# Ends of stages in an encoder layer: x copied first in the first scan step, no state in the last, feed-forward sums behind the first unit, bias rows by one product and a DMA

## What is computed

```
xn = rms_norm(x);  q, k, v, gu, gv, z, xbc, dt, gates = split(xn @ w_in)
y_a = window_attention(q, k, v, ..., rel_bias)      # bias = rel_bias[t5_bucket(key - query)], |key - query| <= 128
y_b = spatial_gating(gu, gv, ...)
y_c = ssd_branch(z, xbc, dt, ...)                   # chunked scan, forward and backward:
    # y_diag = (C B^T * decay) (x dt);  y_off = C state exp(acum);  state = state * decay + B^T (x dt decay_to_end)
h = x + (g_a * y_a @ w_up_attn + g_b * y_b @ w_up_gmlp + g_c * y_c @ w_up_ssd) @ w_out
out = h + square(relu(rms_norm(h) @ w_ff1)) @ w_ff2
```

## Time and profile before

| | us |
|---|---|
| median of 3 runs | 2508.46 |
| lowest, highest | 2508.34, 2509.58 |
| profiled execution, its time | 2509.14 |
| profiled execution, its span | 2507.3 |
| mean granted clock of PE | 0.977 of full speed |

### The profile page before, as it was taken

One profiled execution on the slowest core, in us unless ns is written; L12 is line 12 of the kernel. 1 busy time (PEld: TensorE's weight loads), 2 busy tenths in 40 slices (PEclk: granted clock), 3 DMA queues, 4 the chain that ended last, 5 costly groups with the idle time before them and its releaser, 6 DMA issues. The chain is left out here.

```text
span 2507.3 us, 33471 instructions
## 1 busy us (share of the span) xinstructions
PE 2380.2 (95%) x13080; PEld 1978.2 (79%) x13080; DVE 1109.7 (44%) x1591; ACT 857.2 (34%) x1543; POOL 155.5 (6%) x72
## 2 busy tenths in 40 slices
PE   3999999699998899999879999999999999999999
PEld 1777888576676788888768888788888888888887
DVE  4311164345654566677655543433333333333333
ACT  4431223236655444566543332421121202121120
POOL 3332343100000000000000000000000000000000
PEclk8998999899999999999989999999999999999999
DMA  3121323323223666788574341011111111111112
GB/s 120 38 84 57 123 75 125 98 86 121 92 92 101 192 198 198 217 244 243 177 254 161 91 149 48 29 42 34 42 34 42 33 42 35 40 35 40 38 38 92
DMA packets 170921, 251.04 MB, mean 100 GB/s; under 512 B 10811, under 2 KB 125755, under 8 KB 168156
## 3 DMA queue, kind: packets, MB, share of 16 engines
q1 hardware_dynamic: 170844, 249.99, 31.4%
HBM read 187.47 MB, written 62.49 MB: 100 GB/s over the span
## 5 line engine op out<-in xcount | busy, mean ns | idle before, releaser
L155 PE MATMUL acc<-r_hi,w_hi 128*128 128x512 f32 (+1 forms) x1344 | 478.4, 356 | 21.5 <-DVE r_lo L1652 16.2
L156 PE MATMUL acc<-r_hi,w_lo 128*128 128x512 f32 (+1 forms) x1344 | 477.9, 356 | 0.0
L157 PE MATMUL acc<-r_lo,w_hi 128*128 128x512 f32 (+1 forms) x1344 | 477.2, 355 | 0.0
L155 PEld LDWEIGHTS acc<-r_hi,w_hi 128*128 128x128 f32 x1344 | 255.4, 190 | 59.4 <-issue 22.1
L156 PEld LDWEIGHTS acc<-r_hi,w_lo 128*128 128x128 f32 x1344 | 255.5, 190 | 35.5
L157 PEld LDWEIGHTS acc<-r_lo,w_hi 128*128 128x128 f32 x1344 | 255.1, 190 | 35.8
L156 PE MATMUL acc<-u_hi,w_lo 128*128 128x512 f32 (+1 forms) x768 | 273.7, 356 | 0.0
L155 PE MATMUL acc<-u_hi,w_hi 128*128 128x512 f32 (+1 forms) x768 | 273.6, 356 | 0.0
L157 PE MATMUL acc<-u_lo,w_hi 128*128 128x512 f32 (+1 forms) x768 | 273.6, 356 | 0.0
L195 ACT ACTIVATE w_hi<-w_raw 128x1024 fp32r<-128x1024 f32 x119 | 124.9, 1049 | 386.2 <-PE acc L157 380.1
L155 PE MATMUL acc<-xn_hi,w_hi 128*128 128x512 f32 (+1 forms) x624 | 226.5, 363 | 13.5 <-DVE xn_lo L317 8.8
(11 more groups left out here) (204 smaller groups left out, 3481.3 us busy)
## 6 DMA issues: line engine op xcount, KB each, us to landing
w_raw<-in_w_tiles SPq DMA_DIRECT2D x146, 512.0 KB, 3.7
c_w<-s_ac SPq DMA_DIRECT2D x20, 1024.0 KB, 4.6
c_xbc<-s_xbc_T SPq DMA_DIRECT2D x20, 768.0 KB, 4.8
s_late_T<-s_l_result SPq DMA_DIRECT2D x20, 640.0 KB, 6.8
c_grown<-s_grown SPq DMA_DIRECT2D x40, 256.0 KB, 6.0
gates<-s_late_T SPq DMA_DIRECT2D x16, 512.0 KB, 3.7
s_xbc_T<-x_T_sb SPq DMA_DIRECT2D x12, 640.0 KB, 3.2
s_late_T<-la_result SPq DMA_DIRECT2D x12, 640.0 KB, 3.6
```

Source lines behind the costliest of these rows:

```text
L155: pe.matmul(out, w_hi, x_hi, start=first, stop=False)
L156: pe.matmul(out, w_lo, x_hi, start=False, stop=False)
L157: return pe.matmul(out, w_hi, x_lo, start=False, stop=last)
```

## The change

- Bias rows. The table keeps one column per head, so one product gives the rows of all heads on 8 partitions; DVE copies them once, SP stores them as `bias_row` (8x512, 16 KB) and, after the loop of six xBC tiles, has one DMA from DRAM to DRAM repeat that into `bias_rows` (`spread`). The shifted load moves from there behind the loop of four and behind `store_rows(0)`.
- First scan step. ACT copies x of step 0 before it makes the decays of step 0.
- Last scan step. x_end, kept, the state products and the state sum of step 19 are left out, y's products don't wait for the state, and group 2 of the late tile goes behind them. The last two steps leave PE's loop for that.
- Merge. The first group of `merged` is loaded by eight DMAs, each of one feature block.
- Feed-forward. `sums_of_squares` stands behind the first unit of the first tile, not behind its third.

```diff
@@ project, SP
                 for at, (lo, hi) in enumerate(zip(XBC_CUTS, XBC_CUTS[1:])):
                     kind(F_XBC + 2 * lo, 2 * (hi - lo), xbc_T[2 * lo:2 * hi], ready, 5 + 2 * lo, 1)
                     if at == 0:
-                        rb.shift(sp)
+                        rb.spread(sp)
                         store_scan()
                     else:
                         store_rows(at - 1)
+                    if at == 1:
+                        rb.shift(sp)
@@ RelativeBias
-        self.table = sb("bias_table", [NBUCKET + 1, HEADS, P])
+        self.table = sb("bias_table", [NBUCKET + 1, HEADS])
+        self.row = sb("bias_row", [HEADS, 512])
     def products(self, pe):
         pe.wait_ge(self.filled, 3)
-        for h in range(HEADS):
-            if h >= 2:
-                pe.wait_ge(self.rows_ok, h - 1)
-            pe.matmul(self.summed[:, h % 2], self.table[:, h], self.onehot[:], start=True, stop=True).then_inc(self.rows_summed, 1)
+        pe.matmul(self.summed[0:HEADS, 0], self.table[:], self.onehot[:], start=True, stop=True).then_inc(self.rows_summed, 1)
     def copy_rows(self, dve):
-        for h in range(HEADS):
-            dve.wait_ge(self.rows_summed, h + 1)
-            dve.tensor_copy(self.rows[:, h], self.summed[:, h % 2]).then_inc(self.rows_ok, 1)
+        dve.wait_ge(self.rows_summed, 1)
+        dve.tensor_copy(self.row[:], self.summed[0:HEADS, 0]).then_inc(self.rows_ok, 1)
...
-        sp.wait_ge(self.rows_ok, HEADS)
-        sp.dma_start(self.scratch["bias_rows"], self.rows[:].rearrange("p h r -> p (h r)")).then_inc(self.rows_out, 16)
+        sp.wait_ge(self.rows_ok, 1)
+        sp.dma_start(self.scratch["bias_row"], self.row[:]).then_inc(self.row_out, 16)
+
+    def spread(self, sp):
+        sp.wait_ge(self.row_out, 16)
+        sp.dma_start(self.scratch["bias_rows"], self.scratch["bias_row"].rearrange("(o h) r -> o (h r)", o=1)
+                     .to_broadcast([P, HEADS * 512])).then_inc(self.rows_out, 16)
@@ state_space, PE
-                    pe.wait_ge(c_read, n * 2 + 2)
-                    pe.wait_ge(x_end_ready, n + 1)
-                    for g in range(SG):
-                        cols = slice(g * 512, (g + 1) * 512)
-                        mm = pe.matmul(bank_b[:, cols], b_tok[:, g * SN:(g + 1) * SN], x_end[:, cols], start=True, stop=True)
-                    mm.then_inc(state_full, 1)
+                    if not is_last(n):
+                        pe.wait_ge(c_read, n * 2 + 2)
+                        pe.wait_ge(x_end_ready, n + 1)
+                        for g in range(SG):
+                            cols = slice(g * 512, (g + 1) * 512)
+                            mm = pe.matmul(bank_b[:, cols], b_tok[:, g * SN:(g + 1) * SN], x_end[:, cols], start=True, stop=True)
+                        mm.then_inc(state_full, 1)
                     if d and not (isinstance(n, int) and n == NT):
                         sum_squares(n - 1)
                     late.product(pe, s, n, 1, range(KD // 2, KD))
-                    late.product(pe, s, n, 2)
+                    if not is_last(n):
+                        late.product(pe, s, n, 2)
+                        pe.wait_ge(state_ready, n + 2)
                     pe.wait_ge(x_dt_ready, n + 1)
                     pe.wait_ge(w_ready, n * 2 + 2)
-                    pe.wait_ge(state_ready, n + 2)
                     for h in range(SH):
...
                     mm.then_inc(y_full, 1)
+                    if is_last(n):
+                        late.product(pe, s, n, 2)
...
-                with pe.Fori(NT // 2 + 1, NT) as pair:
+                with pe.Fori(NT // 2 + 1, NT - 1) as pair:
                     for s in range(2):
                         step(s, pair * 2 + s, pair * 64 + 64, 1)
+                for n in (LAST - 1, LAST):
+                    step(n % 2, n, 64 * (n // 2 + 1), 1)
@@ state_space, ACT
                     act.activation(x_tok[:, s], bank_a[:], ACT.Identity).then_inc(x_ready, 1)
+                    if is_first(n):
+                        decays(0, 0, 64, 16, 0)
...
-                decays(0, 0, 64, 16, 0)
                 whole(0)
@@ state_space, DVE
-                    dve.tensor_tensor(heads(x_end[:]), heads(x_tok[:, s]), over_dims(factor(s, S_END, d)), ALU.mult).then_inc(x_end_ready, 1)
+                    if not is_last(n):
+                        dve.tensor_tensor(heads(x_end[:]), heads(x_tok[:, s]), over_dims(factor(s, S_END, d)), ALU.mult).then_inc(x_end_ready, 1)
...
-                    dve.wait_ge(state_ready, n + 1)
-                    dve.tensor_tensor(heads(kept[:]), heads(state[:]), over_dims(factor(s, S_ALL, d)), ALU.mult).then_inc(kept_ready, 1)
+                    if not is_last(n):
+                        dve.wait_ge(state_ready, n + 1)
+                        dve.tensor_tensor(heads(kept[:]), heads(state[:]), over_dims(factor(s, S_ALL, d)), ALU.mult).then_inc(kept_ready, 1)
...
-                    dve.wait_ge(state_full, n + 1)
-                    dve.wait_ge(kept_ready, n + 1)
-                    dve.tensor_tensor(state[:], kept[:], bank_b[:], ALU.add).then_inc(state_ready, 1)
+                    if not is_last(n):
+                        dve.wait_ge(state_full, n + 1)
+                        dve.wait_ge(kept_ready, n + 1)
+                        dve.tensor_tensor(state[:], kept[:], bank_b[:], ALU.add).then_inc(state_ready, 1)
@@ UpProducts, SP
-        for i in range(4):
-            sp.dma_start(m.merged[:, 2 * i:2 * i + 2, 0:512], y_T[2 * i:2 * i + 2, :, 0:512].rearrange("j p t -> p j t")).then_inc(self.ab_in[i], 16)
+        for k in range(KD):
+            sp.dma_start(m.merged[:, k, 0:512], y_T[k, :, 0:512]).then_inc(self.ab_in[k], 16)
@@ FeedForward, PE
                     mm.then_inc(self.full1, 1)
-                if very_first and i == 0:
-                    sums_of_squares()
+                    if very_first and u == 0:
+                        sums_of_squares()
```

More of the change, by code:

```diff
@@ L354, in project @@
                          aux[:].rearrange("p (g n) -> p g n", g=3), "xn", sem, x_in)
-        rb = RelativeBias(ctx, nc, sem, a, scratch, bias, norm.room[:, 0:HEADS])
+        rb = RelativeBias(ctx, nc, sem, a, scratch, bias)
         sums_of = rb.summed[:, :, 0:3 * NT * 16].rearrange("p d (i n) -> p d i n", i=3)
@@ L528, in sums @@
                     pe.wait_ge(dt_step, 3)
-                    pe.wait_ge(rb.rows_ok, HEADS)
+                    pe.wait_ge(rb.rows_ok, 1)
                     for d, kinds in enumerate(((GT, LE, ONES), (LT, GE, ONES))):
@@ L781, with __init__ @@
 class RelativeBias:
-    def __init__(self, ctx, nc, sem, a, scratch, bias, rows):
+    def __init__(self, ctx, nc, sem, a, scratch, bias):
         def sb(name, shape):
             return ctx.enter_context(nc.sbuf_tensor(name, shape, F32))
-        self.a, self.scratch, self.bias, self.rows = a, scratch, bias, rows
+        self.a, self.scratch, self.bias = a, scratch, bias
         self.onehot = sb("onehot_sb", [NBUCKET + 1, 512])
-        self.table = sb("bias_table", [NBUCKET + 1, HEADS, P])
+        self.table = sb("bias_table", [NBUCKET + 1, HEADS])
+        self.row = sb("bias_row", [HEADS, 512])
         self.rel_b = sb("rel_b", [NBUCKET + 1, HEADS])
@@ L795, in __init__ @@
         self.summed = ctx.enter_context(nc.psum_tensor("ps_bias", [P, 2, 512], F32))
-        (self.small_in, self.filled, self.rows_summed, self.rows_ok, self.rows_out, self.shifted_in, self.pads_out) = (
-            sem("rb_" + n) for n in ("small_in", "filled", "rows_summed", "rows_ok", "rows_out", "shifted_in", "pads_out"))
+        (self.small_in, self.filled, self.rows_summed, self.rows_ok, self.row_out, self.rows_out, self.shifted_in,
+         self.pads_out) = (sem("rb_" + n) for n in (
+             "small_in", "filled", "rows_summed", "rows_ok", "row_out", "rows_out", "shifted_in", "pads_out"))
     def load(self, sp):
@@ L808, in fill @@
         dve.wait_ge(self.small_in, 32)
-        dve.tensor_copy(self.table[0:NBUCKET], self.rel_b[0:NBUCKET, :].unsqueeze(2).to_broadcast([NBUCKET, HEADS, P])
-                        ).then_inc(self.filled, 1)
+        dve.tensor_copy(self.table[0:NBUCKET], self.rel_b[0:NBUCKET, :]).then_inc(self.filled, 1)
     def products(self, pe):
         pe.wait_ge(self.filled, 3)
-        for h in range(HEADS):
-            if h >= 2:
-                pe.wait_ge(self.rows_ok, h - 1)
-            pe.matmul(self.summed[:, h % 2], self.table[:, h], self.onehot[:], start=True, stop=True).then_inc(self.rows_summed, 1)
+        pe.matmul(self.summed[0:HEADS, 0], self.table[:], self.onehot[:], start=True, stop=True).then_inc(self.rows_summed, 1)
     def copy_rows(self, dve):
-        for h in range(HEADS):
-            dve.wait_ge(self.rows_summed, h + 1)
-            dve.tensor_copy(self.rows[:, h], self.summed[:, h % 2]).then_inc(self.rows_ok, 1)
+        dve.wait_ge(self.rows_summed, 1)
+        dve.tensor_copy(self.row[:], self.summed[0:HEADS, 0]).then_inc(self.rows_ok, 1)
```

(13 more changed lines are left out.)

1 line of the change is left out of this document (removed).

## The result

The changed kernel takes 2491.51 us (median of 6 runs, 2490.39 to 2492.93) against 2508.18 (6 runs) for the one before: ratio 0.9932, 95% interval 0.9922 to 0.9942. It is 16.7 us faster; forecast were 21, to 2487.7, with a range of 2484.0 to 2493.0. The profiled execution took 2490.52 us with a span of 2488.7, 18.6 us under the span before.

The account below looks back on a forecast made before the run. TensorE, busy 95% of the span, was taken as the bound, with the gaps in its work. Terms -12.1 + 0 - 4.6 - 4.8 + 0 + 0.7 = -20.8 gave 2488.3 us profiled, 2487.7 us median; range 2484.0 to 2493.0.

Parts of the forecast that it names:

- Bias rows: Project stage: one product replaces eight, clock stays high, tile 8's 13th matmul comes earlier, -12.1 us (-9.6 if it falls).
- rival 1: Clock falls behind the bias product too (+2.5) and in the first scan step (+1.1): 2491.3 us; chance 0.16.
- Spread: New 2 MB DRAM-to-DRAM DMA ahead of weight tile 22: takes about the old load's time, 0, upper end +4.7 us.
- Rivals 3 and 4: Spread DMA slow: 3, PE waits 4.7 us for tile 22, 2492.4 us (0.10); 4, 48 us long, 2524 us (0.12).
- First scan step: Scan step 0: copy of x before decays starts y products earlier, -4.6 us, the middle of -5.7 and -3.5.
- Last scan step: Scan step 19: state products go and the last group's narrow matmuls move behind the y products, -4.8 us.
- Feed-forward: Sums behind the first unit: PE idles 6.1 us for DVE's last addition instead of waiting for the root, +0.7 us.
- Merge loads: Merge start: eight 256 KB loads for four of 512 KB, second group's load lands as before; 0, from -0.7 to +2.0 us.
- Rival 5: Merge: the second group slips with its load's later issue, +2.0 us, 2489.7 us; chance 0.06.
- the rule cited beside it: Merge loads: Trainium skill asks at least 1 MiB per DMA for full bandwidth; by it the smaller loads would be slower.

Follow-up runs that it names:

- undo_merge: The changed kernel with the merge's first group loaded by four transfers of 512 KB again instead of eight of 256 KB; 2489.91 us.
- ff_second: The changed kernel with the feed-forward's sums of squares behind the second unit instead of the first; 2486.86 us.
- eight_four: The changed kernel with sums behind the second unit, last addition before the third group's low halves, and merge's second group in four 512 KB loads; 2484.91 us.
- four_four: As eight_four, but with the merge's first group also in four loads of 512 KB instead of eight of 256 KB; 2482.49 us.
- best_mid: As eight_four, with the third merge group's load ahead of the first gates and the sums in the middle of the second unit; 2482.02 us.

## Why the prediction was right in its range, and where it was 3.8 us short

The sum gave 2488.3 us for the profiled execution, which came out at 2490.52, 2.2 us later; the other 1.6 us are the place of the profiled executions among their runs (0.7 us over the median I had before, 1.0 under it after). By its terms:

- *Bias rows*: 12.38 for 12.1. One product, tile 8 at 202.51 at the full clock. That the clock stays high was a choice, and not a safe one: it fell in four of the twelve profiled executions (rival 1's first half).
- *Spread*: 0, as forecast; 9.9 us, under the 8.8 + 3.1 us that would have been covered. Rivals 3 and 4 are out.
- *First scan step*: 5.13 for 4.6, y products at 825.83; with the 10.79 us added by which the stage started earlier, that is 836.6 on the old scale. The closeness is luck, for two errors meet in the row. From the first turn of x the step gained 5.74, my upper end of 5.7, with DVE's chain as described. The clock did fall (0.50 from 822 to 824 us), but I priced that at 2.2 us and took half, and it cost nothing: the y products waited 0.78 us for DVE's state sum and ran at full clock, 1.97 us as before. So this term was 1.1 too small. The 0.61 us ahead of the turn of x hide that.
- *Last scan step*: 4.91 for 4.8.
- *Feed-forward*: +0.07 for +0.7, by the mechanism described: PE waited 5.9 us (6.1 forecast) for DVE's last addition, and tile 1 came at 1608.40, which with the 18.72 us of the earlier start added is 1627.1 on the old scale; forecast 1627.7, against 1627.0 before.
- *Merge loads*: this is the step that failed. I took "it lands when the bytes ahead are through" and **0**; it cost +2.13. The first group gained by the smaller loads 1.3 us where I had 0.65 (4.15 against 5.44 us after the first issue in undo_merge). That more issues do not delay a full queue held up; that the same bytes take the same time did not, since the 256 KB transfers ran slower (306 to 352 GB/s), and an earlier first group only made PE run dry sooner and come back at 1.2 GHz. The second group started 0.8 us later than before, and the low clock in it took the other 1.3. Rival 5 named the place and +2.0, but by the wrong mechanism, its issue; the rule cited beside it had the right one.
- *Not in the sum*: the attention stage's +1.43, a longer stretch of low clock, which kernels with the same code there show in some executions and not in others. With +2.13 and this, and +0.75 - 0.59 of jitter in the first stage, -20.8 becomes -17.1; the other terms, each a little better than forecast (-0.28, -0.53, -0.11, -0.63, and -0.02 in the scan loop), make it -18.65.

The median lies at rival 1's number (2491.3), but not by its way: in the profiled execution the clock stayed up behind the bias product, and its fall in the scan step was hidden. That errors of +3.7 and -1.6 left the time inside the range is in part luck.

## What to carry to other kernels

When a product is moved ahead to hide a chain, move its last input ahead as well: here an addition of 0.42 us, put ahead of eight low halves, made the move behind the first unit worth 5.6 us, and without it that move was worth nothing. Starting a stage's first group earlier helps only as far as its second group follows; smaller loads in front made the one behind later. Look at each wait also for the clock behind it, over several executions: here it fell in four of twelve behind one of 0.6 us. And before a fall is priced, look whether the work under it is waited for: in the first scan step it was not.

## What was unexpected in the hardware

- The same gap has two prices. At PE's wait of 2.05 to 2.45 us before tile 1 the clock fell in four of six executions (ff_second, eight_four, four_four, best_mid) and stayed at 2.4 GHz in two; the feed-forward from the first relu on took 877.8 to 877.9 us in those four and 876.3 in the two. In the attention stage eight of the fourteen profiled executions had one low stretch about 3 us longer than the other six: four of them (the changed kernel, ff_second, four_four, best_mid) behind the gap of 2.7 to 3.1 us for the read-out of a late tile, the other four some 13 us after the stage's start, among narrow score products with waits of 1.1 us. To the first turn of x both took 332.9 to 333.3 us, against 330.9 to 331.2, and nothing between. The runs of one kernel lie up to 6 us apart; how much of that is this was not measured.
- The scan step's fall of the clock cost nothing: the 24 narrow matmuls under it took longer, but the next product waited for DVE.
- A copy of 2 MB from DRAM to DRAM with a broadcast source of 16 KB landed in 9.6 to 11.1 us, in the twelve kernels with it, 0.8 to 2.3 us more than the 8.8 us of a plain load of 1.5 MB before.
- 256 KB transfers back to back moved 306 to 352 GB/s in the changed kernel and 512 KB ones 396 to 410 in undo_merge.
